# Moving 24 small transfers from SyncE's queue to ScalarE's, and reordering some of ScalarE's functions

## The reference, cut to what matters

```python
# fox_mixer
q, k, v, g, z_f = jnp.split(h @ w_in, [D, 2 * D, 3 * D, 4 * D], axis=-1)
q = rmsnorm(q, q_norm_g); k = rmsnorm(k, k_norm_g)          # per head
log_f = jax.nn.log_sigmoid(z_f + b_f)
c = jnp.cumsum(log_f, axis=1)
s = einsum(q, k) * scale + c[query] - c[key]                # causal softmax follows
o = softmax(s) @ v * jax.nn.sigmoid(g)
...
# nsa_mixer: q, kc, vc, ks, vs, kw, vw and gates = x @ w_in
# kc, vc: windows of 32 tokens, a small MLP each -> compressed keys and values
# ks, kw: rotated keys of the selected and of the window branch; softmax attention on each
```

## Time and profile before

| | us |
|---|---|
| three runs | 2217.35, 2220.26, 2220.08 |
| median | 2220.08 |
| the profiled execution | 2217.35 |
| its span, first to last instruction | 2215.6 |
| PE busy | 2099.2 (95%) |
| DVE busy | 1483.9 (67%) |
| ACT busy | 1156.6 (52%) |
| the 128 KB transfers of Nsa, median from issue to landing | 3.1 |
| ACT idle behind the Sigmoid of g1 (L1562, 891.31), for PE | 4.16 |

### The profile page before, as it was taken

How to read it: one execution, slowest core, us unless ns; L and a number is a source line. 1 busy time by engine, 2 the same in 40 slices (tenths; PEclk the granted TensorE clock), 3 DMA queues, 4 the chain that set the end, 5 groups by cost and what they waited for, 6 DMA issues and landing times. The chain is left out here.

```text
span 2215.6 us, 36800 instructions
## 1 busy us (share of the span) xinstructions
PE 2099.2 (95%) x14195; PEld 1884.5 (85%) x14195; DVE 1483.9 (67%) x2248; ACT 1156.6 (52%) x1654; POOL 26.1 (1%) x34
## 2 busy tenths in 40 slices
PE   7999999999999999989999988999999989999997
PEld 6999897999999978779999877788777758778876
DVE  5655675665666644576654456788987466888896
ACT  4343533534444335564433345677776455777774
POOL 1000000000000020000000000000000000000000
PEclk9999999999999999999999979999999999999999
DMA  8555222654444523435554512599995514799991
GB/s 280 190 195 183 96 85 87 222 176 170 171 171 170 191 93 119 149 115 171 185 197 131 173 39 92 192 324 318 358 318 181 218 39 172 246 325 325 317 358 59
DMA packets 312310, 421.09 MB, mean 190 GB/s; under 512 B 7844, under 2 KB 266304, under 8 KB 312096
## 3 DMA queue, kind: packets, MB, share of 16 engines
q1 hardware_dynamic: 311296, 418.09, 55.5%
q0 software_dynamic: 544, 1.62, 0.3%
q10 hardware_dynamic: 384, 0.21, 0.1%
HBM read 416.70 MB, written 1.05 MB: 189 GB/s over the span
## 5 line engine op out<-in xcount | busy, mean ns | idle before, releaser
L2819 DVE TENSOR_TENSOR w_lo<-weight_ring,w_hi 128x1024 fp32r<-128x1024 f32 x384 | 449.2, 1220 | 35.8 <-ACT w_hi L2668 31.2
L569 PE MATMUL banks<-x_hi,w_hi 128*128 128x256 f32 x1408 | 400.7, 285 | 8.6 <-DVE w_lo L522 7.8
L570 PE MATMUL banks<-x_lo,w_hi 128*128 128x256 f32 x1408 | 399.2, 283 | 0.0
L571 PE MATMUL banks<-x_hi,w_lo 128*128 128x256 f32 x1408 | 399.1, 283 | 0.0
L2668 ACT ACTIVATE w_hi<-weight_ring 128x1024 fp32r<-128x1024 f32 x384 | 382.2, 1053 | 21.8 <-PE banks L2555 21.7
L515 ACT ACTIVATE w_hi<-weight_ring 128x1024 fp32r<-128x1024 f32 x88 | 93.0, 1057 | 418.4 <-PE banks L571 418.3
L887 DVE TENSOR_TENSOR pieces<-weight_ring,pieces 128x512 fp32r<-128x512 f32 (+2 forms) x245 | 167.1, 690 | 178.0 <-ACT pieces L876 176.6
L569 PEld LDWEIGHTS banks<-x_hi,w_hi 128*128 128x128 f32 x1408 | 271.0, 192 | 11.0 <-DVE w_lo L522 8.7
L876 ACT ACTIVATE pieces<-weight_ring 128x512 fp32r<-128x512 f32 (+2 forms) x245 | 151.9, 628 | 235.3 <-PE banks L823 233.0
L570 PEld LDWEIGHTS banks<-x_lo,w_hi 128*128 128x128 f32 x1408 | 271.0, 193 | 0.1
L571 PEld LDWEIGHTS banks<-x_hi,w_lo 128*128 128x128 f32 x1408 | 271.0, 192 | 0.0
(11 more groups left out here) (367 smaller groups left out, 3893.0 us busy)
## 6 DMA issues: line engine op xcount, KB each, us to landing
weight_ring<-in_ffn_w_in SPq DMA_DIRECT2D x88, 1024.0 KB, 7.5
weight_ring<-in_moe_w_gate SPq DMA_DIRECT2D x64, 1024.0 KB, 6.4
weight_ring<-in_moe_w_up SPq DMA_DIRECT2D x64, 1024.0 KB, 8.9
weight_ring<-in_moe_w_down SPq DMA_DIRECT2D x64, 1024.0 KB, 10.9
weight_ring<-in_ffn_w_out SPq DMA_DIRECT2D x44, 1024.0 KB, 9.6
weight_ring<-in_hg_w_in SPq DMA_DIRECT2D x12, 1024.0 KB, 8.3
weight_ring<-in_fox_w_in SPq DMA_DIRECT2D x12, 1024.0 KB, 8.6
weight_ring<-in_nsa_w_in SPq DMA_DIRECT2D x10, 1024.0 KB, 7.8
```

The lines of the kernel that those rows point to most:

```text
L569: pe.matmul(out, w_hi, m_hi, start=start, stop=False, skip_group_check=True)
L570: pe.matmul(out, w_hi, m_lo, start=False, stop=False, skip_group_check=True)
L571: return pe.matmul(out, w_lo, m_hi, start=False, stop=stop, skip_group_check=True)
L2819: dve.tensor_tensor(self.piece(s, p, self.w_lo), self.piece(s, p), self.piece(s, p, self.w_hi.bitcast(F32)), ALU.subtract).then_inc(sem[ki ...
```

## The change

It takes the eight `bias_rows` transfers of Fox and the sixteen of Nsa out of SP's queue and puts them, with their waits, into ACT's. In Fox they stand behind the Sigmoid of g3; in Nsa four stand behind each of the copies of kc and vc, and the eight of the keys behind the copy of the compressed keys at q1. In Fox it also changes ACT's order: the root of q comes behind the Sigmoid of g0, and Abs and Exp stand at fox_q2, right ahead of Ln.

```diff
@@ Fox.sp @@
-        eng.wait_ge(self.c_ready, 5)
-        eng.wait_ge(self.bias_ready, 4)
-        for half in range(2):
-            for row, to, src in ((0, self.bq, self.c_hi), (1, self.bq, self.c_lo), (32, self.bk, self.n_hi), (33, self.bk, self.n_lo)):
-                row += half * HD
-                eng.dma_start(to[row:row + 1].bitcast(F32), src[half:FOX_H:2, :].bitcast(F32)).then_inc(self.bias_rows, 16)
         self.sp_out(eng)
@@ Fox.act @@
-            if name == "fox_g0":
-                root("q")
             if part == "g":
                 b.read(act.activation(self.g[:, hs], src, ACT.Sigmoid), name)
...
-            if name == "fox_q0":
-                root("k")
-            if name == "fox_q1":
+            if name in ("fox_q0", "fox_g0"):
+                root("k" if part == "q" else "q")
+            if name == "fox_q2":
 
                 act.wait_ge(self.z_step, 1)
                 act.activation(self.ez, self.zb, ACT.Abs).then_inc(self.z_step, 1)
                 act.wait_ge(self.z_step, 2)
                 act.activation(self.ez, self.ez, ACT.Exp, scale=-1.0).then_inc(self.z_step, 1)
-            if name == "fox_q2":
                 act.wait_ge(self.z_step, 3)
                 act.activation(self.ez, self.ez, ACT.Ln, bias=k.const(C_ONES, 1, FOX_H)).then_inc(self.z_step, 1)
+            if name == "fox_g3":
+
+                act.wait_ge(self.c_ready, 5)
+                act.wait_ge(self.bias_ready, 4)
+                for half in range(2):
+                    for row, to, src in ((0, self.bq, self.c_hi), (1, self.bq, self.c_lo), (32, self.bk, self.n_hi), (33, self.bk, self.n_lo)):
+                        row += half * HD
+                        act.dma_start(to[row:row + 1].bitcast(F32), src[half:FOX_H:2, :].bitcast(F32)).then_inc(self.bias_rows, 16)
@@ Nsa.sp @@
-        for name, once, pairs in (("nsa_kc", self.kc, self.kc2), ("nsa_vc", self.vc, self.vc2)):
-            k.banks.wait_read(eng, name)
-            for j in range(2):
-                src = once[j * HD:(j + 1) * HD]
-                eng.dma_start(pairs[0:HD, j:NSA_KV:2], src).then_inc(self.pairs_placed, 16)
-                eng.dma_start(pairs[HD:P, j:NSA_KV:2, 0:T - 1], src[:, :, 1:T]).then_inc(self.pairs_placed, 16)
         self.sp_blocks(eng, self.then)
-        for n, once, keys in (("ks", self.ks_once, self.ks), ("kw", self.kw_once, self.kw)):
-            k.banks.wait_read(eng, f"nsa_{n}_r")
-            for j in range(2):
-                for half in range(2):
-                    eng.dma_start(keys[half * HD:(half + 1) * HD, j:NSA_KV:2], once[j * HD:(j + 1) * HD]).then_inc(self.keys_placed, 16)
         self.sp_out(eng)
@@ Nsa.act @@
-        for name, once in (("nsa_kc", self.kc), ("nsa_vc", self.vc)):
+        for name, once, pairs in (("nsa_kc", self.kc, self.kc2), ("nsa_vc", self.vc, self.vc2)):
             self.act_pieces(act, self.ahead(name))
             b.read(act.activation(once, two(b.wait(act, name)), ACT.Copy), name)
+            b.wait_read(act, name)
+            for j in range(2):
+                src = once[j * HD:(j + 1) * HD]
+                act.dma_start(pairs[0:HD, j:NSA_KV:2], src).then_inc(self.pairs_placed, 16)
+                act.dma_start(pairs[HD:P, j:NSA_KV:2, 0:T - 1], src[:, :, 1:T]).then_inc(self.pairs_placed, 16)
...
             if name == "q1":
                 src = b.wait(act, "nsa_kcmp")[:, 0:4 * N_CMP].rearrange("p (h n) -> p h n", h=4)
                 b.read(act.activation(self.kcmp_raw, src, ACT.Copy), "nsa_kcmp")
+                for n, once, keys in (("ks", self.ks_once, self.ks), ("kw", self.kw_once, self.kw)):
+                    b.wait_read(act, f"nsa_{n}_r")
+                    for j in range(2):
+                        for half in range(2):
+                            act.dma_start(keys[half * HD:(half + 1) * HD, j:NSA_KV:2], once[j * HD:(j + 1) * HD]).then_inc(self.keys_placed, 16)
```

## The result

The changed kernel takes 2230.74 us, the median of 9 runs (2225.45 to 2236.63); the kernel before, run beside it, 2218.75 (9 runs, 2210.40 to 2220.27). The ratio is 1.0059, with a 95% interval of 1.0047 to 1.0072: slower by about 13 us (10 to 16); the medians are 12.0 apart. The forecast was 2230.5, and slower.

What follows compares the result with a forecast made beforehand. PE, busy 95% of the span, bounds the kernel; what stops it costs time. 3.5 + 1.7 + 1.6 + 1.5 + 0.65 + 1.4 = 10.4 us on the median 2220.08 gives 2230.5, range 2222 to 2236.

Steps and rivals of the forecast that it cites:

- SP's relief at nothing: SP's queue: taking the transfers out gains nothing; Nsa's output weights load at most 11 us earlier, but attention covers it.
- The slack of 1.5 us: Projections: PE waits only for what ACT starts a piece later than 1.5 us after its release; 1.4 in v.
- ACT's price of an issue: Each DMA issue on ACT costs SP's price, about 0.70 us, with 0.27 and 0.88 as ends.
- the cheap rival: All 24 issues: 0.27 us each on ACT, nearly all hidden; 2.5 us stays, 2222.5; chance 0.16.
- q3: Fox, after Abs and Exp move to q2: the next piece is late by 3.0, PE waits 1.5 us (1.1 to 1.9).
- g1: Fox, root of q behind g0's Sigmoid: the reciprocal delays DVE, PE's wait 0.55 becomes 1.2, +0.65 us (0.3 to 1.0).
- v: Fox, behind the eight issues at g3: piece late by 4.9, PE waits 3.5 us (0.3 to 5.3).
- kc: Nsa, behind the four issues after kc's copy: piece late by 2.4, PE waits 0.9 us.
- vc: Nsa, behind the four issues after vc's copy: same pattern as after kc's, PE waits 0.8 us.
- q1: Nsa, behind the eight key issues at q1: piece late by 3.1, PE waits 1.6 us (nothing to 3.8).
- The clock: After PE's wait from the g3 issues: one stretch of 3.3 us at the low clock, +1.4 us (0 to 4).
- The faster rival: Nsa's compressed scores and gates, 1282 to 1302: low-clock stretch runs high, saving up to 8.4 us, 2214.2; chance 0.04.

Runs made afterwards that it cites:

- c: The changed kernel with Fox's eight transfers back on SP, Nsa's sixteen still on ACT; median 2230.17 us, ratio 1.0039 to the kernel before.
- d: The changed kernel with Nsa's sixteen transfers back on SP, Fox's eight still on ACT; median 2226.83 us, ratio 1.0034 to the kernel before.
- e: The kernel before (old order) with all 24 transfers on ACT, one issue behind each piece instead of bursts; 2219.09 us, ratio 0.9997 to before.
- h: The kernel before with only four of Fox's eight transfers on ACT, behind the Sigmoid of g3; one run, 2220.07 us.
- i: The kernel before with Fox's eight transfers on ACT at g3, each cut in two (sixteen issues, same bytes); one run, 2226.47 us.
- f: The changed kernel with twelve dummy matmuls on PE ahead of its wait in v; six runs from 2227.35 to 2240.11 us, ratio 1.0080.

## Why the prediction was right

The mechanism was right, in each of the six places. That 2230.5 and 2230.74 agree to 0.3 us is luck. The forecast started from 2220.08, the median of three runs of before, where nine give 2218.75, and it added 10.4 us where the medians lie 12.0 apart and the ratio gives 13.1 (10.4 to 16). The start was too high and the addition too low, and they cancel. Over 36 runs of the changed kernel the median is 2232.03.

**What bounds the kernel, and SP's relief at nothing: right.** c and d give part of the relief back, and lose nothing by it; e keeps all of it and equals before. The load of the output weights was to go out at most 11 us earlier. Against ACT's copy at q1 (1258.73 before, 1274.18 after) it goes out 11.0 us earlier, and PE gains nothing.

**The slack of 1.5 us, 1.4 in v: right in kind, shown by h and i, and 1.3 in v by them.** At q2 the piece's start was forecast 2.65 + 1.71 = 4.36 us after the Copy's, and is 4.34 after it; the wait there came out 0.2 under the forecast (1.31 beside 1.5), and no row tells whether the release or the slack was off.

**ACT's price of an issue: right.** 0.60 to 0.79 in the rows but for the one of 1.42, 0.65 each in a burst, against 0.70 taken from SP and 0.27 for the cheap rival, which is refuted. The Trainium skill ("DMA: Bandwidth & Descriptors", Issuing engines are not separate DMA queues) calls the sequencer's time usually small beside the DMA. The profile's issue rows after the change (KB each, median us to landing) give the second number:

```profile
arena<-arena ACTq DMA_DIRECT2D x12, 128.0 KB, 2.4
arena<-arena ACTq DMA_DIRECT2D x4, 127.5 KB, 2.8
```

0.65 beside 2.4 to 2.8 is small for the transfer; it isn't for an engine that has 1.5 us to spare and issues eight in a row.

**The terms, forecast and measured:** q3 1.5 and 1.31; g1 +0.65 and +0.71, through the reciprocal as described; v 3.5 and 2.82 to 2.85; kc 0.9 and 1.00 to 1.82; vc 0.8 and 0.92; q1 1.6 and 1.62 to 1.64. In v two small things were off: the issues begin at 913.86, 0.47 ahead of the Sigmoid that they stand behind, where I let them start 0.13 after its start, and eight take 5.4 in place of 5.62. Together that is 0.8 earlier, of which the wait shows 0.65; the slack, 0.1 shorter than assumed, takes up the rest. At q3 the Trainium skill ("ScalarE: Activation LUTs", What ACT_TABLE_LOAD costs) would have added 1.4; the load takes 1.28 in its new place too, and Exp starts right behind. At kc the long fourth issue was not foreseen. The sum of the waits, 8.95 forecast, is 9.25.

**The clock: one stretch of 3.3 us forecast behind v, one of 3.4 found there,** at 1.4 us by the forecast's own rate. That idle time is long enough to lower the clock was taken from two places that disagreed; it held at v, and the same wait of 3.20 near 232 shows that it need not have.

What is over is not explained. The ratio gives 13.1, the waits 9.25; 3.9 is left (1 to 7 by the interval), 2.5 over the forecast's 1.4. In the four profiles themselves nothing is left over: with 8/19 us taken off for each us at the low level, the change's span is 6.8 us longer in the first pair and 10.3 in the second, 8.6 in the mean, beside waits of 9.25 and 8.46. In the runs something is. Over 36 runs of the changed kernel the time grows by 0.40 us for each microsecond at the low level (the level's share worked out from the mean clock; correlation 0.94), close to the 8/19 of the prediction; over 58 runs of before it grows by 0.31. At the same mean clock, from 0.977 to 0.982, the two kernels are 9.5 to 13.1 us apart, about 11 over all of them. So some 2 us over the waits do not follow the mean clock either, and no trace says what they are.

**The faster rival: not seen.** Over the 70 us from 1270 on that hold the compressed scores and the gates, the time at the low level is 31 and 27 us in the two profiles of before, 31 and 24 in those of the change: no gain that outlasts the scatter.

## What to carry to other kernels

An engine that feeds TensorE piece by piece has a slack that two or three rows give (pieces in stock times TensorE's time for one, less the time that a piece needs to be made); price each inserted block against that, not against the engine's busy share, which was 52% here. A DMA issue is an instruction of 0.65 us on the engine that makes it: one behind each piece cost nothing that could be measured, eight in a row cost TensorE 1.6 to 2.9 us. Clearing a queue gains only if someone waited for what stood behind.

## What the runs showed of the hardware that was not expected

- ACT's sequencer issues a DMA while ACT still runs the activation ahead of it (905.02 beside 905.01 in e), even one that has not begun (913.86 against 914.33).
- One issue of 127.5 KB took 1.42 and 1.35 us in two profiles and 0.63 in the other four that have it on ACT behind the copy (the change's second, c, both of f), at the same place.
- The same 128 KB transfers landed in a median of 2.4 us in the six profiles in which ACT issues them in bursts, and of 2.9 to 3.3 in the seven in which SP does. PE gained nothing by it, and why they differ is not shown.
- The same idle time of PE, 3.20 us near 232, was followed by a stretch at the low level in one profile of the kernel before and by none in the other.
- The spread of one kernel's runs (2210 to 2223 for before, 2225 to 2237 for the change) follows the mean granted clock (0.986 to 0.977, and 0.982 to 0.976). Keeping PE busy through its longest new wait removed the low stretch there, and yet four of seven runs had a mean clock of 0.975 to 0.977.
